# The context's products of layer 2 computed between the two layers, three of their weights asked for first

## What is computed

```python
mod = silu(c) @ w_ada + b_ada                        # shift and scale, of the tokens and of the context
h   = modulate(rms_norm(x,   norm_mix_g), sh,  sc)   # 512 x 1024
hc  = modulate(rms_norm(ctx, norm_mix_g), shc, scc)  # 256 x 1024
proj = h @ w_in + b_in                               # u, v, tiny q/k/v, neighbourhood q/k/v, gates
tk_c, tv_c = hc @ w_in[:, tiny k, tiny v] + b        # 64 columns each
nk_c, nv_c = hc @ w_in[:, near k, near v] + b        # 512 columns each
```

## Time and profile before

| | |
|---|---|
| time of the runs, median | 2181.36 us |
| time of the profiled execution | 2187.34 us |
| its span | 2185.5 us |
| PE busy | 1910.1 us (87%) |
| DVE, ACT, POOL busy | 858.6, 551.9, 475.8 us |
| mean granted clock of PE | 0.938 of full |
| PE in the chain that ended last | 71% |
| DMA in that chain | 16% |

### The profile page before, as it was taken

The page is one execution under the profiler, slowest core; times in us unless marked ns, Lnnn a source line. Parts: engine busy times, 40 slices in busy tenths (PEclk is TensorE's granted clock), DMA queues, the critical chain, the costliest instruction groups (busy, mean ns, idle before and its releaser), DMA issues.

```text
span 2185.5 us, 32417 instructions
## 1 busy us (share of the span) xinstructions
PE 1910.1 (87%) x13222; PEld 1296.8 (59%) x13223; DVE 858.6 (39%) x1997; ACT 551.9 (25%) x1026; POOL 475.8 (22%) x523
## 2 busy tenths in 40 slices
PE   5999998759878279899999989899999999999766
PEld 3777787635433168678766657645565555556432
DVE  3154534353221422521477432334444534443226
ACT  4242512311101431412477412201111211111111
POOL 1000000023221100000345000004444544454320
PEclk9998999879999689979999999889999999999998
DMA  8665521359999451211477322348999999999977
GB/s 323 238 244 178 208 117 58 144 195 413 417 418 397 158 141 53 87 23 55 110 147 168 79 105 88 124 174 340 384 405 358 409 407 376 383 381 399 358 281 307
DMA packets 102472, 527.33 MB, mean 241 GB/s; under 512 B 28002, under 2 KB 28306, under 8 KB 48172
## 3 DMA queue, kind: packets, MB, share of 16 engines
q1 hardware_dynamic: 63216, 451.70, 52.3%
q0 software_dynamic: 36256, 64.54, 10.8%
q10 hardware_dynamic: 2844, 8.85, 1.2%
HBM read 519.36 MB, written 51.90 MB: 261 GB/s over the span
## 4 chain that ended last, share of the span: by engine, by line
PE 71%; DMA 16%; DVE 7%; ACT 3%; issue 2%; SPq 0%; POOL 0%; ACTq 0%; POOLq 0%; DVEq 0%
PE ps L251 31%; PE ps L1738 16%; DMA arena<-in_egu 11%; PE ps L1812 8%; DMA arena<-in_ada 3%; PE ps L1704 2%; PE ps L411 2%; PE ps L2942 1%; PE ps L1799 1%; PE ps L433 1%; PE ps L2968 1%; PE ps L2254 1%; DMA arena<-in_bs_row 1%; PE ps L1073 1%; DMA arena<-y_rows 1%
## 5 line engine op out<-in xcount | busy, mean ns | idle before, releaser
L1738 PE MATMUL ps<-arena 128*64 128x256 f32 x4096 | 484.1, 391 | 63.6 <-DMA arena<-in_egu 52.3
L1738 PEld LDWEIGHTS ps<-arena 128*64 128x64 f32 x4096 | 300.2, 141 | 272.0 <-issue 75.8
L251 PE MATMUL ps<-arena 128*128 128x256 f32 (+4 forms) x1268 | 325.3, 418 | 3.3 <-ACT arena L3092 0.9
L251 PEld LDWEIGHTS ps<-arena 128*128 128x128 f32 (+1 forms) x1268 | 228.0, 204 | 84.1 <-issue 63.6
L1686 POOL DMA_INDIRECT arena<-h_rows,arena x160 | 192.2, 1201 | 297.4 <-DVE arena L1667 133.4
L1692 POOL DMA_INDIRECT y_rows<-arena x160 | 160.5, 1003 | 404.7 <-DVE arena L1843 347.2
L1812 PE MATMUL ps<-arena 128*64 128x512 f32 x1024 | 242.2, 602 | 6.5 <-DVE arena L1807 2.5
L1807 DVE COPY arena<-ps 128x256 f32<-128x256 f32 (+1 forms) x96 | 36.5, 380 | 432.8 <-PE ps L1799 432.8
L1786 ACT ACTIVATE arena<-ps 128x256 f32<-128x256 f32 (+1 forms) x96 | 33.5, 349 | 518.6 <-PE ps L1738 518.6
L2906 POOL DMA_DIRECT2D arena<-in_nabias x160 | 85.5, 542 | 356.9 <-PE ps L2771 200.1
L302 DVE TENSOR_TENSOR wlb<-arena,whb 128x1024 fp32r<-128x1024 f32 (+1 forms) x46 | 55.7, 1212 | 195.7 <-ACT whb L294 195.7
(11 more groups left out here) (429 smaller groups left out, 2776.3 us busy)
## 6 DMA issues: line engine op xcount, KB each, us to landing
arena<-in_egu SPq DMA_DIRECT2D x204, 1024.0 KB, 13.4
arena<-in_ed SPq DMA_DIRECT2D x102, 1024.0 KB, 9.6
arena<-in_ada SPq DMA_DIRECT2D x48, 1024.0 KB, 7.0
arena<-in_win SPq DMA_DIRECT2D x33, 1024.0 KB, 5.1
arena<-y_rows SPq DMA_DIRECT2D x20, 1024.0 KB, 13.7
arena<-in_nabias POOLq DMA_DIRECT2D x96, 128.0 KB, 5.6
arena<-in_wout SPq DMA_DIRECT2D x8, 1024.0 KB, 7.2
h_rows<-arena ACTq DMA_DIRECT2D x8, 512.0 KB, 3.6
```

The source lines that it names most:

```text
L251: z = pe.matmul(o, l, r, start=start and i == 0, stop=stop and i == len(pairs) - 1, skip_group_check=check)
L1738: z = pe.matmul(b[64 * j:64 * j + 64, 256 * s:256 * s + 256], XV[:, c, 64 * h:64 * h + 64], wk(k)[:, j * 256:j * 256 + 256], start=k == 0, ...
```

## The change

It computes the context's products (jobs `CTXJ`: blocks 13, 14, 4, 11, 12) on PE in the border, one ahead of each transpose T0 to T3 and the last behind T3. Each has a load of its weights of its own, beside the one that the tokens' product of the same block keeps; those of the first three are issued on SP ahead of the four result tiles, that of block 11 behind the first block of layer 2, and that of block 12 behind the second, once the tiny products are done. The context is loaded within the experts (expert 8), normed in experts 13 and 14, and transposed in experts 16 to 23, to the last 2048 words of `ACC`. The slots NS + 3 and NS + 4 leave the ring behind expert 5 for it, and four later places (`LATER`) come to hold two result tiles and weights. `NKC` and `NVC` move to `GA` and `MSA`, and the bias buffer of even groups to `SCR`, so that its first loads wait for the gating's products. The two loads of bias rows get a semaphore of their own, which is what the value stage's biases wait for. The core of the diff:

```diff
-        L2 = ("late", 6)
+        L2 = ("late", 4)
@@ pe_tokm
-                    w.wait_ge(*l2.to(*L2))
+                    w.wait_ge(*l2.to("bin", 1))
@@ act_l2
-            act.dma_start(BIN[0:1, 0:1216], ...).then_inc(*l2.up("late", "late", 0, by=16))
+            act.dma_start(BIN[0:1, 0:1216], ...).then_inc(*l2.up("bin", "bin", 0, by=16))
...
+            w.wait_ge(*w2.to("ctx0", 4))
+            act.activation(TKC[0:64, :], banks.of(w2, "ck", 4).ap[0:64, 0:256], ACT.Identity, ...)
+            w.wait_ge(*ca.to("y", 3))
+            for i in (11, 12):
+                for j in range(2):
...
+                    act.activation(NKC[:, c, :], banks.of(w2, "ck", i, j).ap[:, 0:256], ...)
@@ pe_experts, act_experts, dve_experts: behind each expert e of layer 1
+                    pe_ctx_turn(pe, w, e)      # act_ctx, dve_ctx
@@
-        RES1 = [2, 3, NS + 3, NS + 4]
+        RES1 = [2, 3, NS + 5, NS + 6]
+        CTXJ, CTXS = [13, 14, 4, 11, 12], [4, 5, NS + 7, NS + 8, NS + 7]
+        def sp_ctx(sp, w, c):
+            i = CTXJ[c]
+            s = ring.turn(w2, ("cw", i), ("ctx", i), [CTXS[c]])
...
+            sp.dma_start(s.ap[:, 0:width2(i)], SRC2[i]).then_inc(*s.up())
@@ sp_xa
-            sp_experts(sp, w, xa)
+            for e in range(xa.E):
+                sp_expert(sp, w, xa, e)
+                if e == 5:
+                    ring.order.remove(CX)
+                    ring.order.remove(HCS)
+                if e == 8:
...
+                    sp.dma_start(cut(s.ap, 2), a["ctx"]...).then_inc(*s.up())
             sp_further(sp, w, xa, fa)
             w.wait_ge(*fa.st.to("over"))
+            for c in range(3):
+                sp_ctx(sp, w, c)
             for t in range(4):
@@ pe_l2
-            for t in range(4):
-                pe_tile_turn(pe, w, nx, t, scr3)
+            CB[:] = [0, 1, 2, 3]
+            for t in range(5):
+                i = CTXJ[t]
+                if i == 4:
+                    pe_ctx_tiny(pe, w)
+                else:
+                    (pe_ctx_feat if i < 13 else pe_ctx_tokm)(pe, w, i)
+                if t < 4:
+                    pe_tile_turn(pe, w, nx, t, scr3)
@@ dve_l2, in the loop over tiles, and behind it
+                if 1 <= t < 3:
+                    w.wait_ge(*w2.to("ctx", 12 + t))
+                    dve.tensor_copy(NVC[:, :, 256 * t - 256:256 * t], ...)
+            w.wait_ge(*w2.to("ctx", 4))
+            dve.tensor_copy(TTC, cut(banks.of(w2, "cv", 4).ap[:, 0:128], 2))
@@ dve_split
+            w.wait_ge(*w2.to("ctx", 14))
@@ sp_w2
+                if i < 2:
+                    sp_ctx(sp, w, 3 + i)
@@ pe_v, pe_qkv: the context's work goes
-                if i == 1:
-                    for k in range(8):
-                        w.wait_ge(*nc_.to("xn", 1))
-                        pe_turn(pe, w, nc_, "n", k, lambda t: CXN[:, t, k * 128:(k + 1) * 128], ("h", k), 2)
...
-                if i >= 11:
-                    pe_ctx_feat(pe, w, i)
...
-                pe_ctx_tokm(pe, w, i, 0, 256, None)
@@ pool_na
-        NBUF = [A[:, o:o + 2048] for o in (GA_AT, TT_AT)]
+        NBUF = [SCR[:, 2048:4096], A[:, TT_AT:TT_AT + 2048]]
...
-                elif n == 1:
+                else:
                     w.wait_ge(*sg.to("mm", 7))
@@ dve_v2
-            w.wait_ge(*na.to("e1", NG - 1, 3))
+            w.wait_ge(*na.to("o", NG - 1))
```

More of the change, by code:

```diff
@@ L89, in up @@
     def up(self):
-        return self.ring.stage.up(f"slot{self.at}", *self.name, by=16)
+        return self.ring.stage.up(f"slot{self.ring.lane.get(self.at, self.at)}", *self.name, by=16)
     @property
@@ L2348, in xt_cols, with act_ctx @@
             return XT[t % 2][:, k * 128:(k + 1) * 128]
[L2350 to L2356, removed]
+        def act_ctx(act, w, e):
+            if e == 13:
+                act_squares(act, w, nc_, "n", [CXT[:, t, :] for t in range(2)], ACC[:, 2048:3072], small[:, 20:22],
+                            lambda i: ring.of(nc_, "ctx").landed)
+                act_root(act, w, nc_, "n", small[:, 22:24])
+            elif e == 14:
+                w.wait_ge(*nc_.to("n", "rstd"))
+                for t in range(2):
+                    w.wait_ge(*nc_.to("n", "sq", t))
+                    act.activation(CXT[:, t, :], CXT[:, t, :], ACT.Copy, scale=small[:, 22 + t:23 + t]).then_inc(*nc_.up("act", "xn", t))
@@ L2481, in pe_w2_tokm, with ctx_weights @@
                 pe_tokm(pe, w, w2, i, q, 0, m, W2S, HP2, bias, width2(i), need=need).then_inc(*w2.up("pe", "mm", i, q))
-        def pe_ctx_tokm(pe, w, i, c0, c1, bias):
-            s = ring.of(w2, "w", i)
+        def ctx_weights(w, i):
+            s = ring.of(w2, "cw", i)
             w.wait_ge(*s.landed)
-            wv = cut(s.ap[:, 0:width2(i)], 8)
-            b = banks.turn(w2, ("cv", i), ("cvout", i))
+            w.wait_ge(*nc_.to("h", 7))
+            return cut(s.ap[:, 0:width2(i)], 8)
@@ L2489, in pe_ctx_tokm, with ctx_bank @@
+        def ctx_bank(w, key, out):
+            b = banks.turn(w2, key, out, CB)
             for f in b.free:
                 w.wait_ge(*f)
-            m = c1 - c0
+            return b.ap
+        def pe_ctx_tokm(pe, w, i):
+            wv = ctx_weights(w, i)
+            b = ctx_bank(w, ("cv", i), ("cvout", i))
             for tt in range(2):
-                z = pe_mm(pe, [(HC[:, k, tt * 128:(tt + 1) * 128], wv[:, k, c0:c1]) for k in range(8)]
-                          + ([] if bias is None else [(ones[0:1, :], bias)]), b.ap[:, tt * m:(tt + 1) * m])
+                z = pe_mm(pe, [(HC[:, k, tt * 128:(tt + 1) * 128], wv[:, k, :]) for k in range(8)], b[:, tt * 256:(tt + 1) * 256])
@@ L2536, in act_v @@
                                        ACT.Gelu).then_inc(*w2.up("act", "tout", i, tp))
-            w.wait_ge(*w2.to("ctx0", 4))
-            act.activation(TKC[0:64, :], banks.of(w2, "ck", 4).ap[0:64, 0:256], ACT.Identity, bias=binc[0:64, 45:46]).then_inc(
-                *w2.up("act", "ckout", 4))
         def dve_v(dve, w):
```

121 lines of the change are left out of this document (70 added, 51 removed).

## The result

| | before | after |
|---|---|---|
| median of the runs made together | 2181.78 us (2178.19 to 2195.04, 6 runs) | 2164.93 us (2155.38 to 2170.35, 6 runs) |
| ratio, 95% interval | 1 | 0.9906 [0.988, 0.9933] |
| span of the profiled execution | 2185.5 us | 2164.3 us |
| mean granted clock of PE | 0.938 | 0.945 |

The change makes the kernel faster by 0.9%: 0.0094 x 2181.8 = 20.5 us by the ratio, 15 to 26 by its interval; the two medians by themselves differ by 16.9, since single runs of one kernel lie up to 17 us apart. The forecast was 24.9 less, near the far end of that interval, and the median lies 8.4 us above the forecast of 2156.5, inside the stated range. The profiled execution took 2166.17 us, 21.2 less than that of before.

What follows compares the result with a forecast made beforehand. It took weight transfers to bound the experts, a chain of small ACT and DVE steps the border, and PE the stretch from 800 us. Terms +2.5 + 10.1 - 37.5 = -24.9 us took 2181.4 to 2156.5 us; range 2147 to 2173.

Steps and rivals of the forecast that it cites:

- Experts, +2.5: Experts of layer 1: loading the 1 MiB context in a stage bound by DMA costs 2.5 us.
- the ring of nine slots: Experts: two of eleven load slots leave the ring; taken as 0, bounds 0 and +5 us.
- Rival D, starved experts: Experts: nine slots don't keep the load queue full, +5 us, 2161.5 us; chance 0.13.
- Rows behind three weights, +6.8: Border's opening: three weights issued ahead of the result rows make the first row 6.8 us late, bounds 5 and 8.
- The split of tile 0, +3.2: Border: DVE's split of tile 0 waits for product 14, chain 3.2 us late, bounds +1.5 and +8.2.
- NVC's copies, and T3: Border: two copies to NVC in DVE's queue add 1.4 us; the last transpose T3 then starts at 778.3.
- Product 12, behind the bank of TKC: Border's end: product 12 waits for a bank ACT frees, starts at 785.1, 6.8 after T3's start, cold, taking 9.7 us.
- First block, 14.7 warm and without the stall: Value stage's first block: no bias stall, 14.7 us warm, ends at 809.5; border as a whole +10.1 us.
- What goes, -37.5: After the border: context transposes, tiny products and products 11 to 14 go from their old places, 37.5 us less.
- Rival C, no full return: Value and query stages: removed products had covered ACT and DVE work (+8), or border weights come late; 2165 us; chance 0.12.
- A: Rival, warm border: PE's clock doesn't fall between the border's products, 2150 us; chance 0.18.
- B: Rival, cold border: the clock stays at 0.50 through every border product, 41 us late there, 2187 us; chance 0.07.

Runs made afterwards that it cites:

- E9: Kernel after with the context loaded a second time within the experts, which nothing reads; experts 280.1 us, 2170.41 us in one run.
- E3: Kernel after with the first result row asked for ahead of the three context weights, and these between the four tiles; 2155.84 us, ratio 0.9857.
- E5: Kernel after with product 13's weights loaded ahead of the border and no context weight sharing the low parts' slot; 2154.67 us, ratio 0.9865.
- E7: Kernel after with 14 idle products, read by nobody, behind product 13 and 14 more behind T3; 2155.76 us, ratio 0.9857.
- E4: Kernel after with product 12 in banks 6 and 7 instead of 2 and 3; 2149.88 us, ratio 0.9843.
- E1: Kernel before with one edit: the bias products wait only for the two loads of bias rows; 2162.63 us, ratio 0.991.
- E8: Kernel after with E3, E4 and E5 together, three copies made earlier and 22 idle products ahead of T0; 2143.45 us, ratio 0.9814.
- E2: Kernel after with the bias products waiting for all late loads again; 2157.43 us, ratio 0.9887.

## Why the prediction was right, and where it was not

**Mechanism and sum: right, with one step half seen.** The four terms of the change sum to -23.7 in the profile, against -24.9; in the second profile of the same kernel to -27.2. Point by point:

- *Experts, +2.5:* 3.5 measured. The load's 2.5 stands by E9 (2.8); the ring of nine slots was put at 0, with bounds 0 and +5, and costs at most 1. Rival D, starved experts, asked for +5 and doesn't hold; the DMA share from 505 to 700 us is 1.01 (before 1.02), so the sign named for it did not come.
- *Rows behind three weights, +6.8:* the first row landed 4.80 us after the border's opening before and 12.04 after (747.01 - 734.97): 7.2. With the row put first it lands 4.8 after the opening again (E3). The size is right.
- *The split of tile 0, +3.2:* DVE waited 2.75 us for product 14 in the list of waits. I had asked for 3 or more. The times hold: T0 came 21.8 us after the border's opening where 21.35 had been worked out (750.4 - 729.03), product 14 ended 32.2 after it (32.1 worked out). But the split is only half of the step. The working doesn't ask when T1 starts, which stands behind product 14 on PE and came 10.2 us after T0 (7.8 before). E5 takes the split's wait away, and the chain is no shorter by it. So the delay belongs to product 14 before T1, whatever DVE waits for.
- *NVC's copies, and T3:* T3 starts 783.93 - 734.97 = 48.96 after the opening; worked out 49.3. From T0 it is 27.2, where 27.9 had been worked out and where it was 23.3 before. With product 14 warm (E7) 24.8 are left, which agrees with the 1.4 of the copies.
- *Product 12, behind the bank of TKC:* 56.6 after the opening; worked out 56.1. It was cold: 9.19 us (9.7). E4 shows that the bank is what it waits for, and E7 that the clock is the rest. The clock rose 4.8 us after T0's and 4.2 after product 12's start; I had taken 5.7, between 3.6 and 8.4, which was too long. The trace of before had a third case that the working left out, the first block's start at 769.07, where the window from 772 to 774 (0.79) puts the rise at 772.8, 3.8 us after it.
- *First block, 14.7 warm and without the stall:* the end came 80.35 us after the opening; worked out 80.5. The 15.6 that the stall's removal was said to have given back is the stall and the cold start together. E1, where the first block still begins cold (9.15 us for its first 60 products, 7.39 warm), gives 13.7 for the stall.
- *What goes, -37.5:* -38.25. PE waits 2.76 us ahead of the first scores, released by ACT, as worked out (2.8). There is no new stop of PE between the query blocks; its longest wait there, 6.8 us for L2789, was in the kernel before too (for L2724). Rival C, no full return, doesn't hold, nor do A and B: T0 and product 12 were cold (against A), and the clock was back 4.8 us after T0's start, within product 14 (against B).

That the border came out within 0.1 us is in part luck: T0 was 0.45 later than worked out, T3 after it 0.8 less late, product 12 behind T3 0.8 later, itself 0.5 shorter, and the first block 0.1, and these cancel.

The Trainium skill (TensorE: Matmul & The Clock Gate, "HAM oscillation — how this bites in real kernels") holds that short bursts between waits each begin cold. The trace agrees for each burst that followed some 5 us without work (T0 after 7.33, product 12 after 6.60, T0 in E8 after 4.63) and not where the gap was short: T0 in E3 (none) and E7 (1.46), product 13 in E8 (2.12 us, then 7.17 us). Rival B's step from there to a border that stays cold throughout failed, since every burst was long enough to rise.

**What was off.** The sum by 1.25 us: +1.0 in the experts, +1.1 behind the first scores, less 0.75 that the middle gave more and 0.1 in the border. The two profiled executions differ by 21.2 us and not by 23.7, since a stretch that the change doesn't touch, up to the experts, took 2.45 us more; in the second profile of the same kernel it took 5.1 less than before. The rest of the 8.4 us between forecast and median isn't accounted for. The spread of the runs is wide enough for it, and the working had no term for that: I put the difference on a median of three runs, as if the change were all that can vary. One mark of the list was off as well: I expected the first row's sum near 743, and it came at 747.03. Of the 3.9 us the stretch ahead of the experts is 2.45, the experts 1.0, the rows 0.4. For the same reason the first block's end came 15.9 later than before and not 12.6, and the first scores 22.3 earlier and not 25.

**What the forecast did not ask:** whether the end of the stall needs the move. It counted the stall's 15.6 us within the border's +10.1, which is right for this kernel; E1 shows that over half as much as the change's gain by stages, 13.8 of 23.7, comes from one wait on more loads than its reader needs, and E2 that the move covers the same stall without that edit.

## What to carry to other kernels

Before work is moved to cover a stall, look at what the stall's semaphore counts: here a wait on two loads instead of seven gave 13.7 us by itself, and the move of five products only some 10 to 13 beside it, by the stages. Work that is moved into a chain of small steps costs what it delays there: its loads ahead of the chain's own (7 us), the next small step on its own engine, which then stands behind it (T1 behind product 14), a bank that it gets only behind another engine's queue (8.35 us, mended by four numbers), and the clock that falls in the gap ahead of it (4.45 us, of which the bank's 8.35 hold 2.1 as well). With the first two mended, the weights of one product asked for earlier and three copies made earlier, the same move together with the mended wait took 42 us off the kernel rather than 20.5 (by the stages 37.9 rather than 23.7).

## What the runs showed of the hardware

*The clock takes different courses in the same program.* Up to the experts all kernels here run the same instructions. PE's first products there start between 448.4 and 458.4 us in twelve profiles, those of two profiles of one kernel 7.5 us apart. In the window of 210 to 225 us the granted clock (the third number from the end) was 1.00 in E1 (whose first products of the experts came at 448.5),

```profile
210.00:225.00 15.00, 13.78 (x124) 11.00 (x128) 8.36 (x10) 5.67 (x8) 0.00 (x0) 1.00 0.58 211
```

0.89 in the kernel after's second profile (450.15),

```profile
210.00:225.00 15.00, 13.08 (x97) 10.45 (x98) 9.06 (x12) 4.93 (x8) 0.00 (x0) 0.89 0.57 211
```

and 0.57 in its first (457.67):

```profile
210.00:225.00 15.00, 12.14 (x71) 9.63 (x72) 10.00 (x12) 5.87 (x10) 0.00 (x0) 0.57 0.58 211
```

In this window PE, DVE and ACT take turns, with PE busy 12 to 14 of 15 us. Of the twelve, the five with 0.89 or more here reach the experts by 452.3, the seven with 0.83 or less at 455.2 or later. What sets the course wasn't tried. It is enough for most of the scatter of the runs (15 us for the kernel after), though only profiled executions show it, and it makes stages of two profiles the better measure of a change of 10 us.

*Products for nothing kept the clock only where the next burst followed closely.* With a gap of 1.46 us (E7) T0 ran at full clock, with one of 4.63 us (E8) at half, though PE had worked for 16.7 us without a stop ahead of it (728.36 to 745.03).

*A cold start costs less than the two levels suggest.* A product of 7.07 us took 8.7 to 9.9 us in all of these kernels when PE had stood idle for 4.9 us or more ahead of it, not 13.8; in the kernel after the clock was back 4.2 to 4.8 us after the start.
